# Projection products that read and write their rows from the last column to the first

## What is computed

```python
for l in range(2):
    x = x + 0.5 * rmsnorm(swiglu(rmsnorm(x, g[0]), w_in, w_out), g[1])      # d_ff 2816
    m = mla(h, ...) if l == 0 else hgrn2(h, ...)                            # h = rmsnorm(x, g[2])
    x = x + rmsnorm(m, g[3])
    x = x + 0.5 * rmsnorm(swiglu(rmsnorm(x, g[4]), w_in, w_out), g[5])

def swiglu(h, w_in, w_out):
    gate, up = jnp.split(h @ w_in, 2, axis=-1)
    return (jax.nn.silu(gate) * up) @ w_out
```

## Time and profile before

| | |
|---|---|
| median of 3 runs | 2029.19 us (2028.70 to 2029.87) |
| the profiled execution: own time | 2032.39 us |
| its span, first to last instruction | 2030.6 us |
| mean granted TensorE clock | 0.997 |
| PE busy | 2020.4 us (100%) |
| PE weight loads busy | 1676.7 us (83%) |
| DVE, ACT, POOL busy | 46%, 35%, 33% |
| HBM traffic | 88 GB/s |

### The profile page before, as it was taken

How to read it: one execution, slowest core, us unless ns; L and a number is a source line. 1 busy time by engine, 2 the same in 40 slices (tenths; PEclk the granted TensorE clock), 3 DMA queues, 4 the chain that set the end, 5 groups by cost and what they waited for, 6 DMA issues and landing times.

```text
span 2030.6 us, 28406 instructions
## 1 busy us (share of the span) xinstructions
PE 2020.4 (100%) x11182; PEld 1676.7 (83%) x11182; DVE 925.3 (46%) x1228; ACT 714.4 (35%) x971; POOL 676.0 (33%) x310
## 2 busy tenths in 40 slices
PE   9999999999999999999999999999999999999999
PEld 7888888888888888888888888888888878888887
DVE  6433421588474343115534311476766766433212
ACT  5222232455342222224222222465655543222221
POOL 4444444220224444442544444200000024444444
PEclk9999999999999999999999999999999999999999
DMA  4233234200223223333232333222221122322332
GB/s 166 93 98 98 91 96 133 95 22 1 63 83 98 99 93 94 99 96 104 78 99 93 96 94 103 81 86 81 68 69 64 64 73 94 99 98 93 96 96 88
DMA packets 54516, 179.49 MB, mean 88 GB/s; under 512 B 6048, under 2 KB 10400, under 8 KB 54432
## 3 DMA queue, kind: packets, MB, share of 16 engines
q1 hardware_dynamic: 54000, 176.73, 27.4%
q10 hardware_dynamic: 432, 1.57, 0.2%
HBM read 176.18 MB, written 2.10 MB: 88 GB/s over the span
## 4 chain that ended last, share of the span: by engine, by line
PE 95%; DVE 2%; ACT 1%; issue 1%; DMA 0%; SPq 0%; DVEq 0%; ACTq 0%
PE psum L637 28%; PE psum L638 28%; PE psum L639 28%; PE psum L793 2%; PE psum L794 1%; PE psum L799 1%; PE psum L1055 1%; PE psum L1162 1%; ACT prob L1666 0%; PE psum L825 0%; PE psum L822 0%; PE psum L1242 0%; PE psum L1199 0%; PE psum L1220 0%; PE psum L1241 0%
## 5 line engine op out<-in xcount | busy, mean ns | idle before, releaser
L563 POOL TENSOR_TENSOR w_lo<-raw,w_hi 128x1024 fp32r<-128x1024 f32 (+1 forms) x276 | 648.9, 2353 | 1302.6 <-ACT w_hi L1459 1302.6
L637 PE MATMUL psum<-xg_hi,w_hi 128*128 128x512 f32 x1735 | 683.4, 394 | 1.0 <-DVE xg_lo L2300 0.5
L639 PE MATMUL psum<-xg_hi,w_lo 128*128 128x512 f32 x1735 | 676.5, 390 | 0.0
L638 PE MATMUL psum<-xg_lo,w_hi 128*128 128x512 f32 x1735 | 676.3, 390 | 0.0
L1459 ACT ACTIVATE w_hi<-raw 128x1024 fp32r<-128x1024 f32 (+1 forms) x332 | 343.1, 1037 | 839.8 <-DMA raw<-w_up 464.1
L637 PEld LDWEIGHTS psum<-xg_hi,w_hi 128*128 128x128 f32 x1735 | 326.2, 188 | 71.2 <-issue 1.6
L639 PEld LDWEIGHTS psum<-xg_hi,w_lo 128*128 128x128 f32 x1735 | 326.2, 188 | 68.5
L638 PEld LDWEIGHTS psum<-xg_lo,w_hi 128*128 128x128 f32 x1735 | 326.3, 188 | 67.1 <-issue 1.2
L637 PE MATMUL psum<-hid_hi,w_hi 128*128 128x512 f32 (+1 forms) x726 | 278.0, 383 | 0.0
L638 PE MATMUL psum<-hid_lo,w_hi 128*128 128x512 f32 (+1 forms) x726 | 277.7, 383 | 0.0
L639 PE MATMUL psum<-hid_hi,w_lo 128*128 128x512 f32 (+1 forms) x726 | 277.7, 383 | 0.0
(11 more groups left out here) (258 smaller groups left out, 1617.0 us busy)
## 6 DMA issues: line engine op xcount, KB each, us to landing
raw<-w_up SPq DMA_DIRECT2D x172, 512.0 KB, 3.5
raw<-w_down SPq DMA_DIRECT2D x64, 512.0 KB, 3.5
raw<-w_hgrn SPq DMA_DIRECT2D x48, 512.0 KB, 3.5
raw<-w_down SPq DMA_DIRECT2D x32, 384.0 KB, 3.1
raw<-w_mla SPq DMA_DIRECT2D x16, 512.0 KB, 3.5
raw<-w_up SPq DMA_DIRECT2D x16, 128.0 KB, 4.6
xt<-x_t SPq DMA_DIRECT2D x8, 256.0 KB, 4.8
out<-xt SPq DMA_DIRECT2D x16, 128.0 KB, 1.7
```

What stands on the lines that cost most here:

```text
L563: pool.tensor_tensor(w_lo[slot][:, 0:n], raw[slot][:, 0:n], w_hi[slot][:, 0:n].bitcast(F32), ALU.subtract).then_inc(w_ready, 1)
L637: first = pe.matmul(ps, w_hi[slot][:, at:at + n], hi, start=start, stop=False)
L638: pe.matmul(ps, w_hi[slot][:, at:at + n], lo, start=False, stop=False)
L639: return first, pe.matmul(ps, w_lo[slot][:, at:at + n], hi, start=False, stop=stop)
```

## The change

A helper builds, for a row of a buffer or of a bank, the same row with its start at the last element and a step of -1. `mm3` applies it to the output and to the two moving operands. The stationary weights are taken as before. The diff in full:

```diff
@@ -461,6 +461,11 @@
             return psum[:, (4, 5, 6, 7)[n], :]
 
+        def backwards(row):
+
+            n = row.shape[1]
+            return bass.AP(tensor=row.tensor, offset=row.offset + n - 1, ap=[list(row.ap[0]), [-1, n]])
+
         def o_gain(head):
             return cols[:, ON_COL + head:ON_COL + head + 1]
 
@@ -634,6 +639,7 @@
             def mm3(ps, w, hi, lo, start, stop):
 
                 slot, at, n = w
+                ps, hi, lo = backwards(ps), backwards(hi), backwards(lo)
                 first = pe.matmul(ps, w_hi[slot][:, at:at + n], hi, start=start, stop=False)
                 pe.matmul(ps, w_hi[slot][:, at:at + n], lo, start=False, stop=False)
                 return first, pe.matmul(ps, w_lo[slot][:, at:at + n], hi, start=False, stop=stop)
```

## The result

The changed kernel takes **2078.16 us** (median of 4 runs, 2077.45 to 2079.98), the one before 2029.53 beside it (4 runs). The ratio is 1.0243, with a 95% interval of 1.0231 to 1.0256: slower by 48.6 us. That lies inside the range, near its middle, and not at the forecast of no change.

The account below looks back on a forecast made before the run. PE starting product after product was taken to bound the kernel. Profiled execution 2032.4 us + 0 for the change = 2032.4; that execution lies 3.2 above the median, so the forecast is 2029.2, range 2026 to 2131.

Parts of the forecast that it names:

- rival 2: Backward projection products pay a part price: fixed cost per product (+100 us, 2129; chance 0.09) or dearer read (2995; 0.03).
- The sign that it named for being wrong: In the changed profile, forward entry rows and backward projection rows show different distances between starts.
- What bounds the kernel: PE starting one product after another: busy 2020.4 of 2030.6 us, 95% of the chain of waits.
- The count of 7362 + 132 products and the spacing of 0.2267 us: Wide and narrow products of the three `mm3` lines; starts of wide ones 0.2267 us apart, 1669 us, 82% of the span.
- By these rows the read should not cost anything: Backward moving read in `mm3` costs nothing, judged from line 1162's batches: 0.76 us for runs of two or more, 0.89 for one.
- Leaves 13.3 ns between two products: Wide `mm3` products: 0.2267 us between starts less 213.3 ns for 512 columns at one per cycle.
- Write: Writing the PSUM row of each projection product from its last column costs nothing; argued, not shown.
- The order of addresses inside a pair should not matter: For a PSUM write that takes two neighbouring words together, falling order costs nothing; argued, not shown.
- rival 1: Backward write breaks the pairing in PSUM, so each product falls to line 735's rate: 1495 us more, 3524; chance 0.16.
- Rival 4: Something between program and chip turns falling rows into rising ones: 2029 as well, counted in the forecast's 0.71.

Follow-up runs that it names:

- the falling groups of four: Changed kernel with rows taken in groups of four, groups in falling order, elements rising inside each, for read and write: 2075.11 us, ratio 1.0226.
- the last probes: Streams of 48 probe products behind the end of the kernel before; plain f32 rows took 0.429 us per record both forward and backward.
- The one-column stream: 12 probe products behind the end of the kernel before, the moving read being one column 512 times: 0.2158 us per product, 518 cycles.

## Why the prediction was half right

Direction and size, first. The forecast was no change, with 0.71; it came slower by 2.4%, in the class that had 0.28. The range held it because rival 2, a small fixed cost per product with a bound of +100 us, was taken in; measured were +48.6. That this is near the middle of the range is luck: no term of the prediction gives 16 cycles. The sign that it named for being wrong came up: in the changed profile the backward rows start 0.2333 us apart and read 397 ns, the forward entries read what they read before.

*What bounds the kernel*: right. PE's starts carry it to the end, and 16 cycles more per product appear in the time undiminished. The count of 7362 + 132 products and the spacing of 0.2267 us are the terms by which the result adds up, to 0.3 us.

*"By these rows the read should not cost anything"*: this step failed. The argument from the earlier trace rows was that a reversed row, like runs of two and more, has neighbours next to each other. It has, and the falling groups of four, four neighbours each, cost the full price all the same. What those rows could not show was named as their weakness and then given too little weight: they are plain f32 records, and the last probes show that at two cycles a column a backward row costs nothing either. They were no witness for a row at one cycle a column. In place of nothing, the read cost 16 cycles, 6.67 ns, in each of 7362 products. The Trainium skill's rule that I set beside them (Advanced Engine Details and Errata, SBUF Cachelines: two hits on a line for full speed) doesn't reach this case: every line is hit four times in both directions, at 544 and 560 cycles.

*"Leaves 13.3 ns between two products"*: misread. I took these 32 cycles for a gap between products, unconnected with the addresses. The one-column stream leaves 6 cycles for that, within 2. The Trainium skill (TensorE: Matmul & The Clock Gate, Back-to-back issue gap) gives an isolated warm product of 512 columns 518 cycles, 2.5 ns beyond its columns; the one-column stream agrees, at 518. The 131 ns per product that the same section gives for a stream are not seen here: none of the fp32r streams of 512 columns took less than 215.8 ns. The other 26 cycles were a cost of the travelling read that the kernel before was already paying, and that was the sign to look for: a product of 512 columns that takes 544 cycles is losing time on something, and an edit that changes the addresses can move that.

*Write*: right. "The order of addresses inside a pair should not matter" is now shown: 2030.41 against 2030.52 us. With it rival 1 falls. The Trainium skill (PSUM — Partial Sum Buffer, Specifications (TRN2)) says that a non-contiguous pattern in PSUM slows matmuls; in these runs a step of -1 costs nothing (ratio 0.9995), so it can't be counted among those patterns. *Rival 4*, a change that doesn't do what it says, falls with the time itself.

*Rival 2*: right in sign and within its bound (48.6 us of 100), wrong in its mechanism. It is not fixed per product, since 256 columns gain 4 cycles, and it is not a charge on runs of one element, since groups of four pay it in full.

*What is shown of the cause, and what isn't.* Shown: the price is the moving read's; with groups of four it depends on the direction in which the groups are taken and not on the step inside them; moving the weights alone by 32 bytes puts the same price on forward rows, with the same gain at 256 columns, moving them by 256 bytes doesn't, and the two prices don't add; a moving read that stands still doesn't pay. For forward rows that ties the price to where the weights are read, and the weight loads go on beside the products (81% of the span in the changed kernel's page) out of the same memory. For backward rows this tie is argued, from the same two marks and the sum that doesn't add: none of 17 shifts, and not even weights at one address, took them below 558 cycles, and no run has backward rows without a weight load beside them. Not shown either is how the two get in each other's way, or why a backward row of 256 is 4 cycles cheaper than a forward one.

## What to carry to other kernels

When PE starts products back to back, compare the distance between starts with the columns at the granted clock: here all but some 6 of the cycles beyond the columns hung on the read. How many they are depends on where the weights and the moving rows lie and on the direction of the walk; the best that these runs found for 512 travelling columns is 544. In this kernel an innocent change of layout by 32 bytes costs 2.3%, so after any change of allocation look at that distance first. In these runs a PSUM row could be written in either direction for free, and groups of four could be reversed inside at no cost to the kernel (0.9998) as long as the groups rose; in the streams, blocks of eight and more could not.

## What was not expected

The same instruction stream ran at 544 or 560 cycles per product depending on the stream ahead of it (weights shifted by 4), steadily over 48 products. Patterns that look tame can be far worse than a reversed row: rising blocks of 16 that fall inside took 640 cycles, groups of four 256 bytes apart 667. And weights read from one and the same address (step 0) cost forward rows 557 cycles, more than weights read in order.
